# Latent attention of a two-layer model: the product of probabilities and values in three fp32r passes over split operands

## What is computed

```
logits = einsum('bqhc,bqkc->bhqk', q_b, kv_sel) * scale     # q_b: queries, width 128
logits = logits + bias; logits = where(valid, logits, -inf)  # bias by distance, per head
probs  = softmax(logits, axis=-1)
o      = einsum('bhqk,bqkc->bqhc', probs, kv_sel)            # the product that is changed
o      = einsum('blhc,hcd->blhd', o, w_uv)
```

## Time and profile before

| | before |
|---|---|
| median of three runs | 3011.16 us |
| the profiled execution | 3012.98 us |
| its span, first to last instruction | 3010.8 us |
| TensorE busy in the span | 2715.2 us (90%) |
| VectorE busy | 1551.6 us (52%) |
| ScalarE busy | 1024.5 us (34%) |
| mean granted TensorE clock | 0.935 |
| latent attention, first to last product | 2035.8 to 2210 us |

### The profile page before, as it was taken

The page is one execution under the profiler, slowest core; times in us unless marked ns, Lnnn a source line. Parts: engine busy times, 40 slices in busy tenths (PEclk is TensorE's granted clock), DMA queues, the critical chain, the costliest instruction groups (busy, mean ns, idle before and its releaser), DMA issues.

```text
span 3010.8 us, 35401 instructions
## 1 busy us (share of the span) xinstructions
PE 2715.2 (90%) x13636; PEld 2058.8 (68%) x13636; DVE 1551.6 (52%) x2160; ACT 1024.5 (34%) x1472; POOL 1020.1 (34%) x264
## 2 busy tenths in 40 slices
PE   5998788999987889999889999899987868799996
PEld 4777747888865468888667766664445746588885
DVE  2736543442356634424353588985525476544244
ACT  3534433322232533222332444534423232332221
POOL 3346613444433023444414333330013433244442
PEclk8999959999998889999999999999997868899998
DMA  4225402222222012222313333342221213122221
GB/s 163 70 85 179 146 30 83 98 98 98 88 99 70 1 56 80 89 97 98 125 60 136 102 105 105 118 141 91 92 104 57 98 50 112 56 88 93 98 98 70
DMA packets 59775, 280.53 MB, mean 93 GB/s; under 512 B 9699, under 2 KB 11325, under 8 KB 32387
## 3 DMA queue, kind: packets, MB, share of 16 engines
q1 hardware_dynamic: 47123, 259.72, 25.6%
q10 hardware_dynamic: 12528, 19.09, 1.7%
HBM read 259.31 MB, written 19.40 MB: 93 GB/s over the span
## 4 chain that ended last, share of the span: by engine, by line
issue 55%; PE 28%; POOL 12%; DVE 3%; ACT 1%; POOLq 0%; ACTq 0%; DVEq 0%
POOL w_lo L2415 10%; PE banks L488 8%; PE banks L490 7%; PE banks L489 7%; PE banks L1241 1%; PE banks L2085 1%; POOL acc L846 1%; PE banks L2095 1%; PE banks L1225 1%; POOL ysd L2160 1%; PE banks L2104 0%; DVE tmp L1566 0%; PE banks L1118 0%; DVE x L1569 0%; PE banks L543 0%
## 5 line engine op out<-in xcount | busy, mean ns | idle before, releaser
L2415 POOL TENSOR_TENSOR w_lo<-raw,w_hi 128x2048 fp32r<-128x2048 f32 x186 | 861.0, 4630 | 1795.6 <-ACT w_hi L467 1714.1
L488 PE MATMUL banks<-hn_hi,w_hi 128*128 128x512 f32 (+1 forms) x2296 | 912.1, 397 | 74.5 <-DVE hn_lo L556 39.1
L490 PE MATMUL banks<-hn_hi,w_lo 128*128 128x512 f32 (+1 forms) x2296 | 908.7, 396 | 0.0
L489 PE MATMUL banks<-hn_lo,w_hi 128*128 128x512 f32 (+1 forms) x2296 | 906.3, 395 | 0.0
L467 ACT ACTIVATE w_hi<-raw 128x2048 fp32r<-128x2048 f32 x182 | 348.1, 1913 | 712.5 <-PE banks L490 677.3
L488 PEld LDWEIGHTS banks<-hn_hi,w_hi 128*128 128x128 f32 x2296 | 439.1, 191 | 197.7 <-issue 74.8
L489 PEld LDWEIGHTS banks<-hn_lo,w_hi 128*128 128x128 f32 x2296 | 439.2, 191 | 97.5 <-issue 1.0
L490 PEld LDWEIGHTS banks<-hn_hi,w_lo 128*128 128x128 f32 x2296 | 439.0, 191 | 93.3
L672 DVE TENSOR_TENSOR hid_lo<-prod,hid_hi 128x512 f32 x66 | 302.1, 4578 | 125.9 <-ACT hid_hi L645 125.9
L490 PE MATMUL banks<-hid_hi,w_lo 128*128 128x512 f32 x528 | 207.6, 393 | 0.0
L489 PE MATMUL banks<-hid_lo,w_hi 128*128 128x512 f32 x528 | 206.4, 391 | 0.0
(11 more groups left out here) (421 smaller groups left out, 3262.7 us busy)
## 6 DMA issues: line engine op xcount, KB each, us to landing
raw<-in_W SPq DMA_DIRECT2D x202, 1024.0 KB, 4.9
spill<-cs ACTq DMA_DIRECT2D x64, 256.0 KB, 3.2
oh<-codes SPq DMA_DIRECT2D x128, 128.0 KB, 2.6
extra<-in_W SPq DMA_DIRECT2D x8, 1024.0 KB, 4.8
grp<-spill SPq DMA_DIRECT2D x8, 512.0 KB, 4.5
grp<-spill SPq DMA_DIRECT2D x16, 256.0 KB, 4.9
zt<-spill SPq DMA_DIRECT2D x8, 512.0 KB, 3.7
x<-in_xT SPq DMA_DIRECT2D x1, 2048.0 KB, 14.1
```

Source lines behind the costliest of these rows:

```text
L488: pe.matmul(out, wh, xh(k), start=(k == 0), stop=False)
L489: pe.matmul(out, wh, xl(k), start=False, stop=False)
L490: mm = pe.matmul(out, wl, xh(k), start=False, stop=(k == nkt - 1))
L2415: pool.tensor_tensor(w_lo[:, u % 2, :], raw[:, u % 2, :], w_hi[:, u % 2, :].bitcast(F32), ALU.subtract).then_inc(S("w_lo"), 1)
```

## The change

The product takes three fp32r matmuls for each of its four parts in place of one float32 matmul: high values times high probabilities, high values times low probabilities, low values times high probabilities. For this
- `kvt` is kept as `kvt_hi` and `kvt_lo`: DVE's copy now rounds, and DVE then subtracts;
- ACT's copy of a turned block writes the rounded `ptt_hi`. It no longer frees the bank; it adds to a new semaphore, `p_turned`;
- DVE forms `ptt_lo`, bank less `ptt_hi`, in a new function `low(m)`, and this frees the bank. `ptt_lo` has one buffer, so low(m) also waits for the product of the group before. It is done in DVE's loop for block n-5, between the maximum of block n and the reciprocal of block n-1, and the loop is four steps longer;
- PE waits, as before, for the last bank of the group to be freed.

```
-            ptt = sb("ptt", [P, 2, NC, T], F32, lat)
+            ptt_hi = sb("ptt_hi", [P, 2, NC, T], F32R, lat)
+            ptt_lo = sb("ptt_lo", [P, NC, T], F32R, lat)
...
-            v.tensor_copy(kvt[:, :, :], chunked(bank(("kvt",))[:, :])).then_inc(reads(("kvt",)), 1)
+            v.tensor_copy(kvt_hi[:, :, :], chunked(bank(("kvt",))[:, :])).then_inc(S("kvt_split"), 1)
+            v.wait_ge(S("kvt_split"), 1)
+            v.tensor_tensor(kvt_lo[:, :, :], chunked(bank(("kvt",))[:, :]), kvt_hi[:, :, :].bitcast(F32), ALU.subtract)\
+                .then_inc(reads(("kvt",)), 1)
...
                     for c in range(NC):
-                        mm = pe.matmul(bank(key)[:, :], kvt[:, c, :], ptt[:, G % 2, c, :], start=(c == 0),
-                                       stop=(c == NC - 1))
+                        ph, pl = ptt_hi[:, G % 2, c, :], ptt_lo[:, c, :]
+                        pe.matmul(bank(key)[:, :], kvt_hi[:, c, :], ph, start=(c == 0), stop=False)
+                        pe.matmul(bank(key)[:, :], kvt_hi[:, c, :], pl, start=False, stop=False)
+                        mm = pe.matmul(bank(key)[:, :], kvt_lo[:, c, :], ph, start=False, stop=(c == NC - 1))
...
+            def low(m):
+                key, G, g = ("ptp", m), m // 4, m % 4
+                v.wait_ge(S("p_turned"), m + 1)
+                if G:
+                    full(v, ("latent", G - 1))
+                v.tensor_tensor(ptt_lo[:, :, g * P:(g + 1) * P], chunked(bank(key)[:, :]),
+                                ptt_hi[:, G % 2, :, g * P:(g + 1) * P].bitcast(F32), ALU.subtract)\
+                    .then_inc(reads(key), 1)
+
             one_hot(0)
-            for n in range(NG + 1):
+            for n in range(NG + 5):
...
-                if n >= 1:
+                if n >= 5:
+                    low(n - 5)
+                if 1 <= n <= NG:
...
-                        a.activation(ptt[:, m // 4 % 2, :, g * P:(g + 1) * P], chunked(bank(key)[:, :]), ACT.Copy)\
-                            .then_inc(reads(key), 1)
+                        a.activation(ptt_hi[:, m // 4 % 2, :, g * P:(g + 1) * P], chunked(bank(key)[:, :]), ACT.Copy)\
+                            .then_inc(S("p_turned"), 1)
```

More of the change, by code:

```diff
@@ L411, in build @@
                 kvf = sb("kvf", [P, T], F32, s5)
-                kvt = sb("kvt", [P, NC, P], F32, s5)
+                kvt_hi = sb("kvt_hi", [P, NC, P], F32R, s5)
+                kvt_lo = sb("kvt_lo", [P, NC, P], F32R, s5)
                 ki = sb("ki", [P, T], F32, s5)
```

## The result

| | before | after |
|---|---|---|
| median of six runs | 3010.69 us | 3078.11 us (3071.2 to 3091.75) |
| the profiled execution, and its span | 3012.98, 3010.8 us | 3071.87, 3070.1 us |
| mean granted clock | 0.935 | 0.931 |
| first maximum to first matmul behind the stage | 2018.4 to 2211.9: 193.5 us | 2014.7 to 2270.5: 255.8 us |

The ratio of the times is 1.0216, with a 95% interval of 1.0194 to 1.0237, so the change costs 65 us (58 to 71); the two medians differ by 67. The prediction was 3065 us, 54 more than before, with a range of 3045 to 3095.

A forecast was written before the change was run, and what follows sets the result against it. PE was taken to bound the stage, busy for all 153.40 us. Waits of 58.5 less 11.2 saved gave +47, with the clock up to +59, middle +53: 3066, on the median 3064, predicted 3065 us, range 3045 to 3095.

The forecast's parts named there:

- What is shorter: Latent attention's product: 3.54 us becomes 2.84, saving 0.70 us a product, 11.2 us in all.
- What is added on DVE: Latent attention: 64 subtractions at 0.69 us, 44 us more; DVE's load about 117 of 153.4 us, still below PE's.
- The ring: Latent attention: PE waits for low, 1.4 us at second transposes, 2.5 before the product; period 14.99 us, +47 us.
- The clock: Latent attention: granted clock between 1.00 and 0.82 slows product and transposes, up to 12 us; the middle taken, +53.
- The early part: Turned values' split in an earlier stage: 0.69 us more on DVE, nobody waits; zero, 4 us in the worst case.
- The sum: Whole kernel: 3013 + 53 = 3066 us, 3064 on the median; 3065 predicted.
- The cover holds: Latent attention: low comes early enough for PE never to wait; 11.2 us saved, 3000 us; chance 0.07.
- The clock stays low: Latent attention: clock at 0.65 makes PE the bound again; +80, 3091 us; chance 0.08.
- The passes aren't as quick: Latent attention's product: each new matmul takes 0.43 us, a product 5.2 us; +85, 3096 us; chance 0.02.

The follow-up runs named there:

- the passes alone: Changed kernel without low; ACT's copy frees the bank, and the second pass reuses the high probabilities. 0.9968 against the kernel before.
- the filled kernel: Changed kernel with nine unneeded bf16 matmuls on PE ahead of each product; 1.0159 against the kernel before, stage 240.2 us.
- both orders: Changed kernel; ACT copies turned blocks before its exponentials, DVE does both subtractions ahead of the odd block's maximum. 0.9966 against the kernel before, 3007.25 us.
- the first experiment: Changed kernel with the three fp32r passes but no subtraction on DVE; 0.9968 against the kernel before, stage 183.8 us.
- low alone: Changed kernel with the fp32 product of the kernel before and unsplit values, DVE's subtraction kept in place; 1.0266 against the kernel before.
- low last: Changed kernel with low(n-5) behind the scaling of block n-1 in place of ahead of the reciprocal; 1.0213 against the kernel before.
- one of the orders changed: Changed kernel with either DVE's subtractions ahead of the even block's maximum, or ACT's turned-block copies ahead of its exponentials; 1.0020 and 1.0052 against the kernel before.
- ACT's order changed: Changed kernel with ACT's copies of the two turned blocks ahead of the two exponentials, DVE's order kept; 1.0052 against the kernel before.
- low twice: Changed kernel with each subtraction of low done twice, the second freeing the bank; one run, 3112.29 us, stage 298.9 us.

## Why the prediction came out as it did

- **What is shorter.** 0.70 us a product was predicted. The changed product starts its matmuls 0.233 us apart (2131.14 to 2131.38 and on), 0.005 more than the projections' 0.228, and the passes alone give 11.79 - 11.16 = 0.63 a period. Right within a tenth; 10 us in all in place of 11.2.
- **What is added on DVE.** 0.69 us each was predicted; the group of 64 has a mean of 687 ns. POOL was idle in the stage, as taken.
- **The ring.** Every station was met within 0.1 us, the two waits are there, and the steady period at full clock is 14.98 for 14.99. The sum of the stage at full clock, +47, is +46.7 by the filled kernel. That the two agree so closely is in part luck: the waits in the profile after are 39.7 + 20.8 = 60.5 us, less the 3.6 us that PE's products waited before, so 56.9 for 58.5, and the saving was 1.1 us too large, which nearly makes up for it. The mechanism was right, and "both orders" shows it from the other side: with the ring opened the same work costs nothing.
- **The clock.** This is the term that was mis-sized. The prediction took a mean clock (1.00 to 0.82), spread it evenly over the PE work on the ring, and took the middle, 6 us. Measured it is 15.6 us (255.8 - 240.2). The mean clock of the stretch is 0.92, which by the prediction's own formula would be (1/0.92 - 1) x 3.53 x 15 = 4.6 us. The step that failed is the even spread. The fall doesn't come just anywhere: in all nine long periods it follows the idle piece before the product and begins 0.3 to 1.5 us after the product's start. In the period shown the last six matmuls of the product then start 0.43 us apart in place of 0.23, and the transposes behind it are slow too. That costs 1.55 us in nine of thirteen periods, 14 us. Of the remaining 1.6 us, 0.7 are in the last interval between products (10.38 us for 9.71 in the filled kernel), and the rest is no clock: it is the 0.06 us by which the filled kernel's periods are shorter. The prediction had cited the Trainium skill ("TensorE: Matmul & The Clock Gate", HAM oscillation), which tells of half rate again and again in a matmul loop that waits for transfers. The trace agrees that the fall comes again and again, with a period of 16.53 in place of 14.98, though the wait here is one for DVE.
- **The early part.** Zero was predicted. In the profile after, the added subtraction runs from 1594.93 for 0.69 us, the next copy starts 1.32 us after that of the values (before, 0.60), so 0.72 us later, and no wait on `kvt_lo` is seen in the profile.
- **The sum.** 47 + 6 = 53 was predicted, 46.7 + 15.6 = 62.3 is the stage in the profile, 65 the ratio. 3078 lies inside the range, 13 us above the forecast; the clock term makes 9 to 10 of them, scatter of the medians the rest as far as can be told.
- **The rivals.** "The cover holds" is wrong for this order and right for the other ones, as it turned out: its own price, 3000, is near what "both orders" measures (10 us below the kernel before). "The clock stays low" did not come: PE never became the bound, because each fall ends behind the product. "The passes aren't as quick" is refuted by the first experiment.

What stays open is why the clock falls in some periods and not in others. It is nine of thirteen in the changed kernel, whose product waits 2.45 us, but eleven in low alone with the same wait, and six with low last and a wait of 2.04. In the kernels with one of the orders changed it is none, and their product waits for 0.76 and 0.89 us only; the timeline's row for the latter, with ACT's order changed:

```profile
2114.22 0.47 PE L1972 MATMUL banks<-ptt_hi,kvt_hi 128*128 128x512 f32 x1 [0.89 <-DVE ptt_lo L1997]
```

## What to carry to other kernels

Before a step is moved from one engine to another, look at where it stands on the new queue, not at how much room that engine has: DVE had 72 us of room in the steady stretch for 36 us of added work (13 periods of four subtractions), and the stage became 47 us longer at full clock because a bank was now freed behind an instruction that waits for the same iteration's matmuls. Walk the chain from a bank's filling to its release once around, with starts from one period of the timeline; here that gave the period to 0.01 us, and those of the other orders to 0.1; it missed by 0.5 where a wait on the same queue (low twice) was left out of the walk. If a change makes PE wait again and again, price the clock on the matmuls right behind the wait, as far as they lie on the ring, at half speed, not as an average over the stage.

## What was not expected of the hardware

- In the changed kernel the fall to 1.2 GHz comes after the wait is over, 0.3 to 1.5 us after the product's start, with 0.43 us from start to start in place of 0.23. In low alone some falls begin up to 0.4 us before the product does.
- Nine useless bf16 matmuls of 512 columns in the idle piece made the stage 15.6 us faster. In the time it is 1.0159 against 1.0216.
- The start of the stage varied from 2011 to 2032 us between executions of kernels that are the same up to there but for one DVE instruction, more than most of the effects studied. The length of the stage repeated to 0.1 us between two kernels with the same period (183.8 and 183.7).
